# A decoder step on one Trainium2 core: the choice of the two experts and their weights moved from VectorE to GpSimd

## The chip, the core and the metric

The kernel runs on one core of a Trainium2 chip. The core has TensorE (PE in the profile; its weight loads are PEld), VectorE (DVE), ScalarE (ACT), GpSimd (POOL), SyncE (SP, here only a queue of DMAs) and 16 DMA engines, which share SBUF and PSUM. Each engine works through its own list of instructions in order and waits on semaphores for the others. The metric is the time of one execution on the device in microseconds; lower is better.

## What is computed

One layer of a decoder for 2048 prompt tokens and 8 decode tokens: a normalised and modulated input goes through one projection into a dilated sliding-window attention and a convolution, both halves are joined and projected out, and a mixture of 32 experts (4 groups of 8; the best group, in it the best 2) follows. The part that matters here, shortened:

```python
x = x + gt1 * (jnp.concatenate([att, conv], axis=-1) @ w_out)
h2 = rmsnorm(x, g_n2) * (1 + sc2) + sh2
lg = hf @ w_rg + b_rg                      # 4 group logits
pg = jax.nn.softmax(lg, axis=-1)
grp = jnp.argmax(lg, axis=-1)
le = (hf @ w_re + b_re).reshape(T, N_GROUPS, EXPERTS_PER_GROUP)[grp]
top_p, top_i = lax.top_k(jax.nn.softmax(le, axis=-1), TOP_K)
wts = p_grp * top_p / jnp.sum(top_p, axis=-1, keepdims=True)
eid = grp[:, None] * EXPERTS_PER_GROUP + top_i
```

Each token's two expert numbers (`eid`), their weights (`wts`) and its rank among the tokens of the same expert are kept; the rank gives the slot that the token's number is written to, from which the experts' stage gathers its rows.

## The kernel before

All matrices are float32, each split into a high and a low part that TensorE multiplies in three products. The kernel runs in stages; the change is in the fourth, `output_projection_and_routing`, between about 903 and 1222 us of the span.

This stage goes over 17 tiles: 16 of 128 prompt tokens and one of the 8 decode tokens. It is a software pipeline: `rounds` calls a body `round_(i)` for i from -1 to 19 on every engine, with i from 3 to 13 as a hardware loop. In round i each engine works on several tiles at once, in the order in which the calls are written:

- TensorE: the projection of tile i (`project`, L2217, 48 matmuls), the turn of the normed rows of tile i-1 (`turn_h2`, L2236), the ranks of tile i-2 (`ranks`, L2254 and L2255: a matmul over the sum `A` of the tile's two one-hot rows, and one over the counts so far), the turn of the convolution of tile i+2 (`turn_conv`, L2189), the turn of the mix of tile i+1 (`turn_mix`, L2206), the logits of tile i-1 (`logits`, L2246).
- VectorE: for tile i-1 the gating of the projection (`gated`, L1990, reads PSUM), for tile i-3 the weights (`weigh`), for tile i-1 the residual add (`added`, L1995), the low part of the turned attention (`att_rest`, L1967), for tile i-2 the logits and the routing (`take_logits`, L2013; `route`, L2027 to L2039), the swish (L1931, YT), for tile i-3 the rank and slot (`rank`), for tile i-2 the choice (`choose`), then the low part of the convolution (`conv_rest`, L1979), the moments of tile i+1 (`moments`, L1960 and L1963, into MV), norm and shift of tile i-1 (L1931 into H2, L1999), and the attention of tile i+1 (`branches`, `branch_shares`, `attended`, the last at L1956 into MIX).
- GpSimd: the kept weights of tile i-3, the scale of tile i-1 (`scale`, L1784, L1786), the normaliser of tile i+1 (`normalise`, L1772 to L1780, waits for the moments), the placing of tile i-3 (`place`: three copies and two indirect DMAs, L1814), the kept expert of tile i-2 (L1799), and inside the loop a DMA of zero rows (L1833). From round 15 on there is no normaliser.
- ScalarE: takes the turned tiles out of PSUM and splits off their high parts, the tanh and swish inputs, the squares (L1877), and for the routing two exponentials (`route_exps`), which give `EV` and `ZG`.

`choose` and `weigh` on VectorE are seven small instructions. `choose` makes the two expert numbers `EID` from the group `GF` and the indices `I8`, their one-hot rows `OH` and the sum `A`, and raises `picked`, for which TensorE's `ranks` and GpSimd's copy wait. `weigh` makes W1 = 1 / ((1 + EV) ZG) and W1 EV, and raises `w_done`. After the last tile the counts become the table of blocks (`experts_table`), with which the stage ends.

Of the kernel before, what the change touches and what calls it, by code (L numbers as in the profile page):

```python
# [17 lines left out]
P = 128  # L18
# [16 lines left out]
PER = 8  # L35
NEXP = GROUPS * PER
# [1556 lines left out]
def output_projection_and_routing(nc, t, dr, const, const_at, state):  # L1593
# [14 lines left out]
    def there(tile, last=TILES):  # L1608
        return not isinstance(tile, int) or 0 <= tile <= last

    def wait(engine, signal, value):
        if not (isinstance(value, int) and value <= 0):
            engine.wait_ge(signal, value)
# [7 lines left out]
    with ExitStack() as ctx:  # L1621
        def sb(name, shape, dt=F32):
            return ctx.enter_context(nc.sbuf_tensor(name, shape, dt))
# [4 lines left out]
        sem = stage_semaphores(nc, ctx)  # L1628
# [7 lines left out]
        BM, BE, BW, BT, BD, BRC = (sb("BM", [P, HEADS]), sb("BE", [P, 3, HEADS]), sb("BW", [P, 3, HEADS]), sb("BT", [P, 3, HEADS]), sb("BD", [P, HEADS]), sb("BRC", [P, HEADS]))  # L1636
        BS, MV, VE, RS, YT, TH = sb("BS3", [P, 6]), sb("MV3", [P, 2]), sb("VE3", [P, 1]), sb("RS3", [P, 1]), sb("YT3", [P, KC, P]), sb("TH3", [P, KC, P])
        MIX, MTH, MTL = sb("MIX", [P, D]), sb("MT_H", [P, KD, P], F32R), sb("MT_L", [P, KD, P], F32R)
        HA = KD // 2
# [10 lines left out]
        weight_kept, rank_kept, expert_kept, slot_copied = sem("weight_kept"), sem("rank_kept"), sem("expert_kept"), sem("slot_copied")  # L1650
        placing = sem("placing")
        NOROWS = sb("NOROWS", [P, D])
        BR = sb("BR", [P, NR])
# [24 lines left out]
        x2_out, h2_out, slot_out, count_psum, count_ready = sem("x2_out"), sem("h2_out"), sem("slot_out"), sem("count_psum"), sem("count_ready")  # L1678
        DECT = TILES

        with nc.Block() as block:
# [80 lines left out]
            def _(pool):  # L1762
                pool.iota(state["token"][:], [[P, ALLT]], base=0, channel_multiplier=1).then_inc(preset, 1)
                pool.memset(CNT[:], 0.0).then_inc(preset, 1)
                pool.memset(G8[:], -3e38).then_inc(preset, 1)
                pool.memset(NOROWS[:], 0.0).then_inc(norows_set, 1)
                for n in range(2):
                    pool.memset(SUMS[n][:], 0.0).then_inc(preset, 1)
# [19 lines left out]
                def column(name, i):  # L1788
                    return state[name][:, i:i + 1] if isinstance(i, int) else state[name][:, ds(i, 1)]

                def keep_weight(i):
                    pool.wait_ge(w_done, i + 1)
                    pool.sem_inc(placing, 1)
                    pool.tensor_copy(column("weight", i), W1[:, None, :]).then_inc(weight_kept, 1)

                def keep_expert(i):
                    pool.wait_ge(picked, i + 1)
                    pool.sem_inc(placing, 1)
                    pool.tensor_copy(column("expert", i), EID[:, None, :]).then_inc(expert_kept, 1)  # L1799

# [16 lines left out]
                def round_(i):  # L1817
                    if there(i - 3):
                        keep_weight(i - 3)
                    if there(i - 1):  # L1820
                        scale(i - 1)
                    if there(i + 1, TILES - 1):
                        normalise(i + 1)
                    if there(i - 3):
                        place(i - 3, rows_of(i - 3))
                    if there(i - 2):
                        keep_expert(i - 2)
                    if not isinstance(i, int):

                        pool.wait_ge(norows_set, 1)  # L1830
                        first = pool.snap(i * (3 * P) + (NEXP - 3 * 3) * P)
                        pool.sem_inc(placing, 1)
                        pool.dma_start(dr["y"][ds(first, 3 * P)].rearrange("(b p) d -> p b d", p=P),  # L1833
                                       NOROWS[:, None, :].to_broadcast([P, 3, D])).then_inc(norows_out, 16)

# [5 lines left out]
            def _(act):  # L1841
# [10 lines left out]
                def take_conv(i):  # L1852
                    if isinstance(i, int) and i == DECT:

# [28 lines left out]
                def route_exps(i):  # L1883
                    act.wait_ge(gmax_ready, i + 1)
                    nc.scalar.activation(GE[:], LOG[:, 0:GROUPS], ACT.Exp, bias=NG[:], scale=1.0, accum_out=ZG[:]).then_inc(group_exp, 1)
                    act.wait_ge(gap_ready, i + 1)
                    nc.scalar.activation(EV[:], DV[:], ACT.Exp).then_inc(gap_exp, 1)
# [41 lines left out]
            def _(dve):  # L1929
# [84 lines left out]

                RST = 9

                def route(i):
# [3 lines left out]
                    def step(ins):  # L2021
                        at[0] += 1
                        ins.then_inc(rstep, 1)
                        dve.wait_ge(rstep, i * RST + at[0])

                    dve.wait_ge(logits_taken, i + 1)
                    step(nc.vector.tensor_copy(G8[:, 0:GROUPS], LOG[:, 0:GROUPS]))  # L2027
                    nc.vector.memset(PAUSE[:], 0.0)
# [11 lines left out]
                    assert at[0] == RST  # L2040

                def choose(i):
                    nc.vector.tensor_copy(I2[:], I8[:, 0:2]).then_inc(cstep, 1)
                    dve.wait_ge(cstep, i * 5 + 1)
                    wait(dve, expert_kept, i)
                    stt(EID[:], GF[:].to_broadcast([P, 2]), float(PER), I2[:], ALU.mult, ALU.add).then_inc(cstep, 1)
                    dve.wait_ge(cstep, i * 5 + 2)
                    nc.vector.tensor_tensor(OH[:], const("iota")[:, None, :].to_broadcast([P, 2, NEXP]), EID[:, :, None].to_broadcast([P, 2, NEXP]), ALU.is_equal).then_inc(cstep, 1)
                    dve.wait_ge(cstep, i * 5 + 3)
                    nc.vector.tensor_tensor(A[:], OH[:, 0], OH[:, 1], ALU.add).then_inc(picked, 1)  # L2050

                def weigh(i):
                    dve.wait_ge(gap_exp, i + 1)
                    wait(dve, weight_kept, i)
                    stt(DEN[:], EV[:], 1.0, ZG[:], ALU.add, ALU.mult).then_inc(cstep, 1)
                    dve.wait_ge(cstep, i * 5 + 4)
                    nc.vector.reciprocal(W1[:, 0:1], DEN[:]).then_inc(cstep, 1)
                    dve.wait_ge(cstep, i * 5 + 5)
                    nc.vector.tensor_tensor(W1[:, 1:2], W1[:, 0:1], EV[:], ALU.mult).then_inc(w_done, 1)

# [67 lines left out]
                def round_(i):  # L2128
                    if there(i - 1):
                        gated(i - 1, rows_of(i - 1), which_of(i - 1))  # L2130
                    if there(i - 3):
                        weigh(i - 3)
                    if there(i - 1):
# [8 lines left out]
                    if there(i - 3):  # L2142
                        rank(i - 3, rows_of(i - 3))
                    if there(i - 2):
                        choose(i - 2)
                    if isinstance(i, int) and i == 0:
# [785 lines left out]
```

## Time and profile before

| | before |
|---|---|
| median of 3 runs | 2150.32 us |
| lowest, highest | 2149.15, 2156.6 us |
| the profiled execution, its own time | 2152.61 us |
| span of its instructions | 2151.1 us |
| busy: PE, PEld | 1979.5 us (92%), 1587.9 us (74%) |
| busy: DVE, ACT, POOL | 1564.6 us (73%), 1051.0 us (49%), 530.8 us (25%) |

The span runs from the first to the last instruction of the profiled execution. Shares over the whole span mix stages with different limits, so the stage of the change is read by itself: in windows (busy time of each engine in a stretch) and in timelines (an engine's instructions in order of time, equal ones merged, with the idle time ahead of them and what ended it in brackets).

### The profile page before, as it was taken

Reading aid. Unit: us, or ns where it says so; the run is one execution under the profiler, and the core shown is the slowest. Engines: PE = TensorE matmul, PEld = TensorE weight load, DVE = VectorE, ACT = ScalarE, POOL = GpSimd, SP = SyncE. Lnnn points to the kernel's source line nnn. Section 1 sums busy time; section 2 is a strip of 40 time slices with the busy share of each in tenths; the row PEclk is TensorE's granted clock in tenths of the full one; section 3 lists DMA queues with packets and bytes.
Section 4 is the critical chain, followed back from the end, with each engine's and each line's share of the span. In section 5 each row is a group of like instructions: output and inputs, shape, how many; then the busy total and the mean of one; then the engine's idle time right before and its main releaser. Section 6 shows DMA issues by size and latency. Waiting matters only on the chain. (4 is left out here: it accounts for less than half of the span.)

```text
span 2151.1 us, 40123 instructions
## 1 busy us (share of the span) xinstructions
PE 1979.5 (92%) x13273; PEld 1587.9 (74%) x13274; DVE 1564.6 (73%) x3061; ACT 1051.0 (49%) x2056; POOL 530.8 (25%) x569
## 2 busy tenths in 40 slices
PE   5999999998999999689999499999999999999986
PEld 3788888886787777378888478788787877878732
DVE  2648898887788888289998678664637576558747
ACT  2411111111888888045444277555536575557533
POOL 1013454331111144015564300101010101000155
PEclk8999999999999999789999699999999999999978
DMA  8786555674759488767877299974848798769967
GB/s 255 240 289 247 186 195 188 210 254 146 234 149 309 151 286 293 239 220 231 275 251 270 78 347 398 343 292 179 295 163 327 267 360 306 273 223 395 391 222 310
DMA packets 221489, 553.19 MB, mean 257 GB/s; under 512 B 28978, under 2 KB 43658, under 8 KB 220105
## 3 DMA queue, kind: packets, MB, share of 16 engines
q1 hardware_dynamic: 171131, 425.60, 56.5%
q0 software_dynamic: 25024, 75.71, 9.7%
q10 hardware_dynamic: 25239, 50.67, 6.8%
q8 instruction: 52, 0.85, 0.2%
q14 instruction: 43, 0.35, 0.1%
HBM read 456.95 MB, written 167.56 MB: 290 GB/s over the span
## 5 line engine op out<-in xcount | busy, mean ns | idle before, releaser
L2546 DVE TENSOR_TENSOR LO<-WIDE,HI 128x2048 fp32r<-128x2048 f32 x128 | 287.1, 2284 | 82.2 <-ACT HI L2468 82.2
L647 DVE SCALAR_TENSOR_TENSOR arena<-arena,tapw 128x512 f32<-128x512 f32 (+3 forms) x435 | 266.3, 690 | 0.0
L2468 ACT CAST HI<-WIDE 128x2048 fp32r<-128x2048 f32 x128 | 238.5, 1910 | 24.0 <-PEq L220 15.7
L448 POOL TENSOR_TENSOR STATS<-STATS,K 128x1 f32<-128x1 f32 x16 | 135.2, 8451 | 308.4 <-ACT H L500 308.4
L2546 DVE TENSOR_TENSOR LO<-W2E,HI 128x2048 fp32r<-128x2048 f32 x64 | 143.8, 2288 | 92.1 <-ACT HI L2468 92.1
L780 PE MATMUL PJ<-WIN_H,HTH 128*128 128x512 f32 x640 | 160.5, 393 | 5.0 <-ACT HTH L508 5.0
L790 PE MATMUL PJ<-WIN_L,HTH 128*128 128x512 f32 x640 | 158.7, 390 | 0.0
L784 PE MATMUL PJ<-WIN_H,HTL 128*128 128x512 f32 x640 | 158.2, 389 | 0.0
L2468 ACT CAST HI<-W2E 128x2048 fp32r<-128x2048 f32 x64 | 118.8, 1904 | 60.1 <-issue 60.1
L780 PEld LDWEIGHTS PJ<-WIN_H,HTH 128*128 128x128 f32 x640 | 118.8, 188 | 33.1 <-issue 9.2
L532 ACT ACTIVATE arena<-PJ 128x512 f32<-128x512 f32 x48 | 28.6, 601 | 231.6 <-PE PJ L790 231.6
L784 PEld LDWEIGHTS PJ<-WIN_H,HTL 128*128 128x128 f32 x640 | 120.2, 188 | 25.2
L790 PEld LDWEIGHTS PJ<-WIN_L,HTH 128*128 128x128 f32 x640 | 119.8, 188 | 25.5 <-issue 0.8
L2421 POOL DMA_INDIRECT XG<-h_rows,IDX x40 | 44.8, 1121 | 366.2 <-PE XP L2605 338.3
L1281 PE MATMUL TB<-K,PR 128*128 128x128 f32 x600 | 81.1, 278 | 8.6 <-ACT PTS L1163 8.2
L2621 PE MATMUL YP<-HI,GH 128*128 128x512 f32 x320 | 84.1, 405 | 4.6
L1176 ACT ACTIVATE PR<-MOD_,ML 128x256 f32<-128x256 f32 (+1 forms) x192 | 86.5, 461 | 1.3 <-PE TB L1281 0.8
L2834 PE MATMUL SUM<-Y,SHARE 128*128 128x512 f32 (+1 forms) x136 | 69.7, 665 | 18.4 <-DMA Y<-expert_rows,dest 16.1
L2616 PE MATMUL AE<-HI,XH 128*128 128x512 f32 x320 | 80.3, 393 | 6.8 <-issue 6.8
L2506 ACT CAST GH<-GP 128x256 fp32r<-128x256 f32 x80 | 29.8, 372 | 114.8 <-PE GP L2611 112.3
L1176 ACT ACTIVATE PR<-SBX,ML 128x256 f32<-128x256 f32 (+1 forms) x192 | 85.8, 453 | 0.0
L2417 POOL DMA_DIRECT2D IDX<-slot_tokens x40 | 23.1, 576 | 247.4 <-issue 247.4
(375 smaller groups left out, 4489.4 us busy)
## 6 DMA issues: line engine op xcount, KB each, us to landing
WIDE<-in_w_expert_gate SPq DMA_DIRECT2D x64, 1024.0 KB, 8.4
WIDE<-in_w_expert_up SPq DMA_DIRECT2D x64, 1024.0 KB, 9.9
W2E<-in_w_expert_down SPq DMA_DIRECT2D x64, 1024.0 KB
expert_rows<-YE ACTq DMA_DIRECT2D x40, 512.0 KB, 6.2
expert_rows<-NOROWS POOLq DMA_DIRECT2D x11, 1536.0 KB
QN<-q_rows SPq DMA_DIRECT2D x48, 256.0 KB
KN<-out_new_k_prompt SPq DMA_DIRECT2D x48, 256.0 KB, 4.9
VN<-out_new_v_prompt SPq DMA_DIRECT2D x48, 256.0 KB, 4.7
```

Source lines behind the costliest of these rows:

```text
L448: pool.tensor_tensor(MS[:], SSQ[:], const("eps"), ALU.add).then_inc(ms_ready, 1)
L647: ins = nc.vector.scalar_tensor_tensor(out=out, in0=src, scalar=tap, in1=out, op0=ALU.mult, op1=ALU.add)
L780: nc.tensor.matmul(PJ[:, n], HTH[:, k], WH[:, n, k], start=k == 0, stop=False)
L784: nc.tensor.matmul(PJ[:, n], HTL[:, k], WH[:, n, k], start=False, stop=False)
L790: mm = nc.tensor.matmul(PJ[:, n], HTH[:, k], WL[:, n, k], start=False, stop=k == KD - 1)
L1176: ins = nc.scalar.activation(PR[hh][:, h, 0:w], SBX[hh][:, h, 0:w], ACT.Exp, bias=ML[g.q][:, head:head + 1], scale=-1.0, accum_out=ML[g.q] ...
L1281: mm = nc.tensor.transpose(TB[u % 2][:, n], PR[head // HH][:, head % HH, k * P:(k + 1) * P], const("ident"))
L2468: nc.scalar.copy(HI[n][:, cols], raw[n][:, cols]).then_inc(hi_ready[n], 1)
L2546: nc.vector.tensor_tensor(LO[n][:, cols], raw[n][:, cols], HI[n][:, cols], ALU.subtract).then_inc(lo_ready[n], 1)
L2616: mm = nc.tensor.matmul(out, x[:, k], w[n][:, k * DEXP:(k + 1) * DEXP], start=first and k == 0, stop=last and k == KD - 1)
L2621: mm = nc.tensor.matmul(YP[:, half * 512:half * 512 + 512], g[:, k], w[2][:, k * D + half * 512:k * D + half * 512 + 512], start=first and ...
L2834: mm = nc.tensor.matmul(SUM[0:r, n % SUMS, cols], SHARE[0:r, n % SUMS, which, 0:r], y[0:r, n % DEEP, cols], start=which == 0, stop=which == 1)
```

## The change

`choose` and `weigh` leave VectorE's program. GpSimd does both for tile i-2, at the end of its round, behind the placing of tile i-3, and keeps expert and weight right behind each. The weights are now made one round earlier in program order than before. GpSimd's forms are simpler, so there are more: `choose` is the cast of the indices, the group times 8, their sum (EID), two one-hot comparisons of 32 columns, their sum (A), and the copy of the expert; `weigh` is an add, a product, a power of -1, a product, and the copy. VectorE's `route` gets a wait for `picked` of the tile before, ScalarE's `route_exps` one for `w_done` of the tile before. A tile of 128 bytes per partition (MIXPLACE), which nothing reads or writes, lies ahead of MIX, MT_H and MT_L, so these and all behind them lie 128 bytes further; four small tiles and two semaphores are added.

```diff
@@ -1635,6 +1635,7 @@
+        PLACED = sb("MIXPLACE", [P, 32])
         MIX, MTH, MTL = sb("MIX", [P, D]), sb("MT_H", [P, KD, P], F32R), sb("MT_L", [P, KD, P], F32R)
...
@@ -1788,14 +1795,43 @@
-                def keep_weight(i):
+                def weigh(i):
+
+                    pool.wait_ge(gap_exp, i + 1)
+                    pool.sem_inc(placing, 1)
+                    pool.tensor_tensor(ONEPLUS[:], EV[:], const("ones")[:, 0:1], ALU.add).then_inc(weigh_step, 1)
+                    pool.wait_ge(weigh_step, i * 3 + 1)
+                    pool.tensor_tensor(DEN[:], ONEPLUS[:], ZG[:], ALU.mult).then_inc(weigh_step, 1)
+                    pool.wait_ge(weigh_step, i * 3 + 2)
+                    wait(pool, weight_kept, i)
+                    pool.sem_inc(placing, 1)
+                    pool.tensor_tensor(W1[:, 0:1], DEN[:], MINUS[:], ALU.pow).then_inc(weigh_step, 1)
+                    pool.wait_ge(weigh_step, i * 3 + 3)
+                    pool.tensor_tensor(W1[:, 1:2], W1[:, 0:1], EV[:], ALU.mult).then_inc(w_done, 1)
                     pool.wait_ge(w_done, i + 1)
                     pool.sem_inc(placing, 1)
                     pool.tensor_copy(column("weight", i), W1[:, None, :]).then_inc(weight_kept, 1)
 
-                def keep_expert(i):
-                    pool.wait_ge(picked, i + 1)
+                def choose(i):
+
+                    pool.wait_ge(rstep, i * RST + RST)
                     pool.sem_inc(placing, 1)
+                    pool.tensor_copy(I2[:], I8[:, 0:2]).then_inc(cstep, 1)
+                    pool.tensor_tensor(GROUP8[:], GF[:], EIGHT[:], ALU.mult).then_inc(cstep, 1)
+                    pool.wait_ge(cstep, i * 5 + 2)
+                    wait(pool, expert_kept, i)
+                    wait(pool, slot_ready, i)
+                    pool.sem_inc(placing, 1)
+                    pool.tensor_tensor(EID[:], I2[:], GROUP8[:].to_broadcast([P, 2]), ALU.add).then_inc(cstep, 1)
+                    pool.wait_ge(cstep, i * 5 + 3)
+                    wait(pool, kstep, i * 2)
+                    pool.sem_inc(placing, 1)
+                    for n in range(2):
+                        pool.tensor_scalar(OH[:, n], const("iota"), EID[:, n:n + 1], None, ALU.is_equal).then_inc(cstep, 1)
+                    pool.wait_ge(cstep, i * 5 + 5)
+                    wait(pool, counted, i)
+                    pool.sem_inc(placing, 1)
+                    pool.tensor_tensor(A[:], OH[:, 0], OH[:, 1], ALU.add).then_inc(picked, 1)
                     pool.tensor_copy(column("expert", i), EID[:, None, :]).then_inc(expert_kept, 1)
...
@@ -1815,8 +1851,6 @@
                 def round_(i):
-                    if there(i - 3):
-                        keep_weight(i - 3)
                     if there(i - 1):
                         scale(i - 1)
...
                     if there(i - 2):
-                        keep_expert(i - 2)
+                        choose(i - 2)
+                        weigh(i - 2)
...
@@ -1882,6 +1917,7 @@
                     act.wait_ge(gmax_ready, i + 1)
+                    wait(act, w_done, i)
...
@@ -2024,6 +2058,7 @@
                     dve.wait_ge(logits_taken, i + 1)
+                    wait(dve, picked, i)
...
```

VectorE's own `choose` and `weigh` (L2042 to L2059 of the kernel before) and their two calls in its round go.

VectorE, the first round behind the loop (rounds inside it read alike but for register rows), from the swish to the moments, before:

```order
L1931 SCALAR_TENSOR_TENSOR YT<-TH,YT 128x512
L2064 TENSOR_TENSOR CNT<-CNT,AR 128x32
L2065 TENSOR_TENSOR RSEL<-OH,SMALL 128x64
L2068 TENSOR_REDUCE R<-RSEL 128x2
L1931 SCALAR_TENSOR_TENSOR SLOT<-EID,R 128x2
L2043 CAST I<-I 128x2
L1931 SCALAR_TENSOR_TENSOR EID<-GF,I 128x2
L2048 TENSOR_TENSOR OH<-K,EID 128x64
L2050 TENSOR_TENSOR AR<-OH 128x32
L1979 TENSOR_TENSOR MT_L<-YT,MT_H 128x512
L1960 BN_STATS BS<-CP 128x6
```

and after:

```order
L1967 SCALAR_TENSOR_TENSOR YT<-TH,YT 128x512
L2080 TENSOR_TENSOR CNT<-CNT,AR 128x32
L2081 TENSOR_TENSOR RSEL<-OH,SMALL 128x64
L2084 TENSOR_REDUCE R<-RSEL 128x2
L1967 SCALAR_TENSOR_TENSOR SLOT<-EID,R 128x2
L2015 TENSOR_TENSOR MT_L<-YT,MT_H 128x512
L1996 BN_STATS BS<-CP 128x6
```

The four instructions of the choice are gone; the three of the weights, between L1990 and L1995, are gone likewise.

GpSimd, inside the loop, from the placing to the DMA of zero rows, before (ISA and REGISTER_ALU rows are its sequencer's waits and sums):

```order
L1808 COPY SLOTP<-SLOT 128x2
L1809 REGISTER_ALU
L1809 COPY rank<-R 128x2
L1814 DMA slot_tokens<-TOK,SLOTP 69632x1 x2
L1797 REGISTER_ALU
L1799 ISA
L1799 COPY expert<-EID 128x2
L1833 ISA
L1833 DMA expert_rows<-NOROWS 128x3x1024
```

and after, from the same two DMAs to the sum that TensorE waits for, and the first of the weights:

```order
L1850 DMA slot_tokens<-TOK,SLOTP 69632x1 x2
L1817 ISA
L1819 CAST I<-I 128x2
L1820 TENSOR_TENSOR GROUP<-GF,PERGROUP 128x1
L1821 ISA
L1825 TENSOR_TENSOR EID<-I,GROUP 128x2
L1826 REGISTER_ALU
L1613 REGISTER_ALU
L1830 TENSOR_SCALAR OH<-K,EID 128x32 x2
L1831 REGISTER_ALU
L1834 TENSOR_TENSOR AR<-OH 128x32
```

The choice now comes behind the two DMAs of the placing. TensorE's order is what it was: its rank matmul over AR stands between the turn of the normed rows and the turns of the convolution and of the mix.

## Rows read from the trace of the kernel before

**Rows 1.** Windows: busy us (instructions) of each engine; granted clock, DMA share, GB/s.

```profile
1000.00:1100.00 100.00, 98.35 (x559) 83.83 (x558) 94.40 (x290) 47.75 (x117) 57.73 (x88) 1.00 0.78 257
```

**Rows 2.** Timeline, TensorE, a steady round: start us, us, instruction, [idle <-releaser].

```profile
1062.46 0.31 PE L2254 MATMUL SMALL<-AR,K 128*128 128x32 f32 x2
...
1063.75 1.06 PE L2206 MATMUL TPS<-K,MIX 128*128 128x128 f32 x8 [0.29 <-issue]
```

**Rows 3.** Timeline, TensorE, the first round with a rank, and tile 12's rank.

```profile
967.05 0.31 PE L2254 MATMUL SMALL<-AR,K 128*128 128x32 f32 x2
...
968.76 1.87 PE L2246 MATMUL SMALL<-WR,H2T 128*128 128x36 f32 x16
...
981.69 1.04 PE L2236 MATMUL HPS<-K,H 128*128 128x128 f32 x8
982.56 0.31 PE L2254 MATMUL SMALL<-AR,K 128*128 128x32 f32 x2
...
1158.49 0.31 PE L2254 MATMUL SMALL<-AR,K 128*128 128x32 f32 x2
```

**Rows 4.** Timeline, VectorE, a steady round.

```profile
1048.75 0.15 DVE L1931 SCALAR_TENSOR_TENSOR DEN<-EV,ZG 128x1 f32<-128x1 f32 x1
...
1049.21 1.23 DVE L1995 TENSOR_TENSOR X<-X 128x1024 f32<-128x1024 f32 x1
...
1050.95 0.18 DVE L2013 TENSOR_TENSOR LOG<-SMALL,BR 128x36 f32<-128x36 f32 x1
...
1054.69 0.16 DVE L2043 CAST I<-I 128x2 f32<-128x2 uint32 x1
...
1055.46 0.69 DVE L1979 TENSOR_TENSOR MT_L<-YT,MT_H 128x512 fp32r<-128x512 f32 x1
...
1056.80 0.18 DVE L1963 BATCH_NORM_AGGREGATE MV<-BS 128x2 f32<-128x6 f32 x1
...
1062.96 0.69 DVE L1956 TENSOR_TENSOR MIX<-NB 128x512 f32<-128x512 f32 x1
1063.60 1.23 DVE L1990 TENSOR_TENSOR X<-OP,GATE 128x1024 f32<-128x1024 f32 x1
```

**Rows 5.** Timeline, GpSimd, the same round.

```profile
1057.06 1.18 POOL L1772 TENSOR_TENSOR VE<-MV,K 128x1 f32<-128x1 f32 x1 [2.28 <-DVE MV L1963]
...
1063.44 1.05 POOL L1814 DMA_INDIRECT slot_tokens<-TOK,SLOTP  x1 [0.31 <-issue]
1064.49 0.20 POOL L1799 COPY expert<-EID 128x2 f32 x1
...
1065.56 0.92 POOL L1794 COPY weight<-W1R 128x2 f32 x1
1069.43 0.71 POOL L1784 TENSOR_TENSOR MS<-SSQ,K 128x1 f32<-128x1 f32 x1 [2.96 <-ACT SQ L1877]
```

**Rows 6.** GpSimd: timeline with VectorE idle; groups by form (busy us, mean ns | idle).

```profile
912.09 0.19 POOL L1772 TENSOR_TENSOR VE<-MV,K 128x1 f32<-128x1 f32 x1 [6.88 <-DVE MV L1963]
912.35 0.55 POOL L1775 TENSOR_TENSOR RS<-VE,K 128x1 f32<-128x1 f32 x1
...
L1038 POOL TENSOR_TENSOR DPR<-dec_k,WAD 128x768 f32<-128x768 f32 x8 | 14.6, 1819 | 12.2 <-DVE SC L1085 12.2
```

**Rows 7.** Timeline, TensorE, behind an idle time in the experts' stage.

```profile
2044.15 0.69 PE L2611 MATMUL GP<-K,GE 128*128 128x128 f32 x2 [2.71 <-DVE GE L2565]
...
2045.40 3.02 PE L2621 MATMUL YP<-HI,GH 128*128 128x512 f32 x8
2048.25 2.00 PE L2621 MATMUL YP<-HI,GL 128*128 128x512 f32 x8
```

**Rows 8.** Timelines, TensorE and GpSimd, last tile.

```profile
1210.26 0.63 PE L2254 MATMUL SMALL<-AR,K 8*128 8x32 f32 x2 [4.08 <-DVE AR L2050]
...
1212.81 0.19 POOL L1799 COPY expert<-EID 128x2 f32<-128x2 f32 x1
```

More of the change, by code:

```diff
@@ L1651, in output_projection_and_routing @@
         placing = sem("placing")
+        EIGHT, MINUS, ONEPLUS, GROUP8 = sb("PERGROUP", [P, 1]), sb("MINUSONE", [P, 1]), sb("ONEPLUS", [P, 1]), sb("GROUP8", [P, 1])
+        amounts_set, weigh_step = sem("amounts_set"), sem("weigh_step")
         NOROWS = sb("NOROWS", [P, D])
@@ L1679, in output_projection_and_routing @@
         DECT = TILES
+        RST = 9
         with nc.Block() as block:
@@ L1766, in _ @@
                 pool.memset(NOROWS[:], 0.0).then_inc(norows_set, 1)
+                pool.memset(EIGHT[:], float(PER)).then_inc(amounts_set, 1)
+                pool.memset(MINUS[:], -1.0).then_inc(amounts_set, 1)
+                pool.wait_ge(amounts_set, 2)
                 for n in range(2):
@@ L2013, in take_logits @@
                     nc.vector.tensor_tensor(LOG[:], LP[:], BR[:], ALU.add).then_inc(logits_taken, 1)
-                RST = 9
                 def route(i):
@@ L2040, in route @@
                     assert at[0] == RST
[L2042 to L2059, printed above, removed]
                 def rank(i, rows):
@@ L2130, in round_ @@
                         gated(i - 1, rows_of(i - 1), which_of(i - 1))
-                    if there(i - 3):
-                        weigh(i - 3)
                     if there(i - 1):
@@ L2143, in round_ @@
                         rank(i - 3, rows_of(i - 3))
-                    if there(i - 2):
-                        choose(i - 2)
                     if isinstance(i, int) and i == 0:
```

## The prediction

> **What bounds the kernel now.** I read the windows by engine first, then the timelines of the stage "output projection and routing" (903 to 1222 us of the span) engine by engine. The windows show that TensorE and VectorE are both nearly full there, at the full clock, while GpSimd has 42% of its time free [rows 1]. That invites moving small VectorE work to GpSimd. The timelines say who holds the round. The stage runs one round per tile of 128 tokens. I count rounds by the start of the rank matmul: tile 0's at 967.05, tile 12's at 1158.49, twelve rounds in 191.4 us, 15.95 us each [rows 3]. TensorE pauses once in a round, before it turns the mix: that starts at 1063.75, 0.1 us after VectorE has ended the mix (1062.96 + 0.69) [rows 2, 4]. In the first of the twelve rounds this pause is absent, and TensorE needs 15.51 us to the next rank matmul (967.05 to 982.56 [rows 3]). VectorE's rows show no gap in a steady round. So VectorE is the bound by a small margin: 15.95 against TensorE's 15.51. Shortening VectorE can save at most 0.44 us a round, some 5 us over the twelve.
>
> **What leaves VectorE.** The three instructions of the weights take 0.46 us (1048.75 to 1049.21) and the four of the choice 0.77 us (1054.69 to 1055.46) [rows 4]. That is 1.23 us a round, nearly three times the 0.44 it can be paid for.
>
> **What comes onto GpSimd, and where.** The choice of tile i-2 now stands behind the placing of tile i-3, whose two indirect DMAs end at 1064.49 [rows 5]. But TensorE wants the rank matmul of that very tile at 1062.46 [rows 2], 2.0 us before GpSimd even begins, and this matmul reads the sum of the one-hot rows that the choice produces. Before, VectorE had it ready at 1055.46. Behind the waiting rank matmul TensorE's queue holds the turn of the convolution, the turn of the next mix, the logits and the next projection. So a new wait stands in the main chain, and it feeds itself: logits release VectorE's routing, that reaches the moments, those release GpSimd's normalise, then the placing, then the next choice. I add up this loop from one rank matmul, at r, to the next:
> - TensorE, rank to end of logits: 967.05 to 968.76 + 1.87, 3.6 us [rows 3].
> - VectorE, logits taken to moments ready: 1050.95 to 1056.80 + 0.18 is 6.03 us, less the 0.77 of the choice: 5.26, so r + 8.9 [rows 4].
> - GpSimd, moments ready to the end of the second indirect DMA: 1056.98 to 1064.49, 7.5 us, r + 16.4 [rows 5]. Nothing in it changes, since VectorE does beside it what it did before.
> - The choice. The trace has no such GpSimd instructions, so I bound it. A free GpSimd instruction on one or two columns takes 0.19 us [rows 6]; 768 columns take 1.82 us, so 32 columns add 0.07. Seven instructions in five dependent steps, 0.08 us between steps, come to about 1.3 us. That is the lower end. But GpSimd's small instructions are held while VectorE runs a large operation on two operands in SBUF: the same kind of first step takes 1.18 us beside one and 0.19 free, and the copy of the weights takes 0.92 us beside the residual add (which began at 1065.2, as it did at 1049.21 one round before) [rows 4 to 6]. The copy of the expert, beside the gating that reads PSUM, is not held: 0.19 [rows 5]. The gating starts at 1063.60 [rows 4] and, with the weights gone, the residual add follows 1.25 us later, at 1064.85 to 1066.08. The first two instructions fit in front of it, the third (the expert's number) would start at about 1064.9 and is held to 1066.1; the one-hot rows and their sum then take 0.8 with VectorE idle. End at 1066.9: 2.4 us. I take this, as the copy of the weights is the nearest row. As upper end I take 3.0.
> - TensorE starts within 0.1.
>
> The sum is 3.6 + 5.26 + 7.5 + 2.4 + 0.1 = 18.9 us a round instead of 15.95. Twelve rounds: 227 less 191.4, **+35 us**. The weights on GpSimd (five instructions, one of them a power at 0.55 us, some 1.8 in all) lie behind the choice; GpSimd then waits for ScalarE's squares, as it does today for 2.96 us [rows 5], with 2.9 us more in the longer round, so they cost nothing. ScalarE's new wait for the weights is 5 us behind them. VectorE's new wait before routing is for a choice that TensorE has already waited for.
>
> The last rounds have no normalise, so GpSimd comes to the choice early: tiles 13 and 14 find no wait, and the round to tile 13 drops its pause, -0.8 us. The last tile waits again: its rank matmul started at 1210.26, right after VectorE's choice, while GpSimd ends placing at 1212.81 [rows 8] and needs 1.3 us for the choice: 1214.1, +3.8 us, and the block table is behind it. Together without the clock: 35.4 - 0.8 + 3.8 = **+38 us**.
>
> The Trainium skill (GPSIMD Engine Reference, section 4.1, Engine selection) puts two-input elementwise work on GpSimd at about twice VectorE's time. By that the choice would take 2 x 0.77 = 1.5 us, a round 18.0, and the sum without the clock would be some +28 us; the held copy in this trace speaks for more than a factor of two, and the row decides.
>
> **The clock.** TensorE ends turning the normed rows at r + 14.64 + 1.04 = r + 15.7 [rows 3], so it would idle 3.2 us in every round. After an idle time of 2.71 us the next matmuls ran at the lower level: eight 512-column ones took 3.02 us against 2.00 us for the next eight, and the six transposes ahead of them 1.25 against about 0.8; some 1.5 us lost, then full speed again [rows 7]. I take the 0.8 from the eight transposes of the normed rows, 1.04 us at the full clock [rows 3]. What follows the idle time here (rank, turns, logits) is the part of TensorE's work that is on the loop, the projection behind it has slack. I take 1.5 us in four of five rounds, about 14 us (all twelve: 18; none: 0).
>
> **The mix tile's move** by 128 bytes changes no instruction and no count; TensorE's eight transposes and the two writers of that tile show no row that depends on where it lies. I take 0; on TensorE's projection even a few ns per matmul would now be hidden by the idle time.
>
> **Forecast.** 38 + 14 = +52 us. The profiled execution took 2152.61 us (span 2151.1), 2.3 above the median of 2150.32 of three runs; against the median, **2202 us**.
>
> **Rivals.**
> 1. The clock stays up, since the idle time is short of what lets it fall each time. For it: a round has 15 us of dense matmuls. Against it: the row of 2.71 us [rows 7]. 2150.3 + 38 = 2188 us.
> 2. GpSimd is not held in the choice (its instructions slip in between VectorE's): 1.3 us, a round of 17.8, TensorE idle 2.1 us. Twelve rounds +22, with the ends +25: 2175 us. The tight start of the third instruction speaks for it, the copy at 0.92 against it.
> 3. Not slower: the choice is ready before TensorE asks. It decides at 1062.46; GpSimd would have to end placing by 1061.1 instead of 1064.49. If the placing shrank by 3.4 us with a freer VectorE, TensorE alone would set the round: 12 x 0.45 = 5 us less, 2145 us. Against it: the two DMAs overlap the same VectorE work as before, as the loop gives VectorE nothing to skip there.
> 4. Each step on GpSimd is dearer than its rows (one-hot with a per-partition scalar, which no row shows): choice 3.0 us and the clock down in each round: 19.5 + 1.5, some +64: 2214 us; at 0.3 us more in each of its steps, 2222.
>
> **Chances.** Forecast 0.54, rival 1 0.22, rival 2 0.08, rival 3 0.05, rival 4 0.11. A measurement of this kernel tells a change from none at about 0.5%, 11 us. Only rival 3 is within that or faster: slower 0.95, same 0.04, faster 0.01. The range from 2174 to 2222 takes in rivals 1, 2 and 4 and leaves out rival 3 and the tails.
>
> **What would show it.** Right: TensorE's rank matmul waits about 3 us for GpSimd's AR in every round from tile 1 to 12; the rounds are 18 to 21 us long; the expert's number on GpSimd takes over 1 us; VectorE has gaps before the high-low split of the mix; the granted clock of the stage falls below 1.0; outside the stage nothing moves. Wrong: rounds of 15.5 us with no idle time ahead of the rank matmul would mean that the placing ends sooner than I say; no slow logits after the idle time would give the clock's 14 us back; a choice of over 3 us would mean that I priced GpSimd's instructions too low.

## The result, and the profile after

| | before | after |
|---|---|---|
| median | 2151.64 us (4 runs) | 2231.38 us (4 runs) |
| lowest, highest | 2149.15, 2156.6 us | 2229.16, 2237.38 us |
| the profiled execution, its own time | 2152.61 us | 2237.38 us |
| span of its instructions | 2151.1 us | 2235.8 us |

The ratio is 1.037, 95% interval 1.034 to 1.040: slower by 80 us, where I had forecast 52 (2202 us) and at most 72 (2222 us). The direction and the place were right, the size was not. The profiled execution of after is the slowest of its four, 6 us above their median, so its rows add up to 85 us more than before, not 80.

The page of after: span; busy time, share and instructions of each engine.

```profile
span 2235.8 us, 40327 instructions
...
PE 2017.2 (90%) x13273; PEld 1624.9 (73%) x13274; DVE 1552.9 (69%) x2942; ACT 1051.5 (47%) x2056; POOL 570.9 (26%) x741
```

GpSimd has 40 us more to do and VectorE 12 less. TensorE is 38 us "busier" with the same work, which means that part of it ran at the lower clock. Windows of the stage, before and then after, and 100 us in its middle, after (columns as in [rows 1]):

```profile
903.00:1222.00 319.00, 276.25 (x1495) 233.74 (x1495) 271.81 (x811) 130.68 (x304) 140.67 (x234) 0.92 0.69 228
```

```profile
905.00:1310.00 405.00, 317.07 (x1495) 273.12 (x1495) 259.30 (x691) 130.63 (x304) 185.97 (x406) 0.81 0.54 180
1000.00:1100.00 100.00, 86.14 (x400) 74.55 (x400) 67.01 (x184) 31.95 (x80) 51.97 (x106) 0.85 0.51 176
```

In the middle, where TensorE and VectorE were nearly full [rows 1], VectorE now has a third of its time free and TensorE 14%; the granted clock has gone from 1.00 to 0.85. The waits of after from 950 to 1230 us say for what (us in total, times, longest):

```profile
PE SMALL L2266 <- POOL AR L1834: 39.1, 12, 4.6
...
DVE LOG L2049 <- PE SMALL L2258: 16.7, 13, 2.0
```

TensorE's rank matmul waits twelve times for GpSimd's sum of the one-hot rows in this stretch: 0.42 us for tile 0, then 0.90 to 4.61 for tiles 1 to 11 (tile 12's, 2.75, lies behind it). Over tiles 1 to 12 that is 3.45 us on average, and 0.90 and 2.16 in two of the rounds. One round in the timeline of TensorE, after:

```profile
1037.17 0.63 PE L2266 MATMUL SMALL<-AR,K 128*128 128x32 f32 x2 [4.54 <-POOL AR L1834]
...
1038.92 1.92 PE L2218 MATMUL TPS<-K,MIX 128*128 128x128 f32 x8
1040.63 3.47 PE L2258 MATMUL SMALL<-WR,H2T 128*128 128x36 f32 x16
1043.90 3.27 PE L2229 MATMUL OP<-WO_H,MT_H 128*128 128x512 f32 x8
1047.01 2.01 PE L2229 MATMUL OP<-WO_H,MT_L 128*128 128x512 f32 x8
...
1056.11 1.03 PE L2248 MATMUL HPS<-K,H 128*128 128x128 f32 x8
1060.25 0.63 PE L2266 MATMUL SMALL<-AR,K 128*128 128x32 f32 x2 [3.10 <-POOL AR L1834]
```

Behind the idle time the transposes (1.92, in [rows 2] 1.06), the logits (3.47, in [rows 3] 1.87) and most of the first eight projection matmuls (3.27) run at about half speed. VectorE in the same round, up to the moments, and its gating and residual add:

```profile
1044.22 0.20 DVE L2049 TENSOR_TENSOR LOG<-SMALL,BR 128x36 f32<-128x36 f32 x1 [1.97 <-PE SMALL L2258]
...
1049.46 0.18 DVE L1999 BATCH_NORM_AGGREGATE MV<-BS 128x2 f32<-128x6 f32 x1
...
1056.49 1.23 DVE L2026 TENSOR_TENSOR X<-OP,GATE 128x1024 f32<-128x1024 f32 x1 [0.17 <-PE OP L2229]
1057.75 1.22 DVE L2031 TENSOR_TENSOR X<-X 128x1024 f32<-128x1024 f32 x1
```

GpSimd in the same round, from the second indirect DMA to the sum:

```profile
1056.14 1.01 POOL L1850 DMA_INDIRECT slot_tokens<-TOK,SLOTP  x1 [0.30 <-issue]
1057.17 0.19 POOL L1819 CAST I<-I 128x2 f32<-128x2 uint32 x1
1057.32 0.18 POOL L1820 TENSOR_TENSOR GROUP<-GF,PERGROUP 128x1 f32<-128x1 f32 x1
1057.70 0.19 POOL L1825 TENSOR_TENSOR EID<-I,GROUP 128x2 f32<-128x2 f32 x1 [0.20 <-POOL GROUP L1820]
1058.19 1.37 POOL L1830 TENSOR_SCALAR OH<-K,EID 128x32 f32<-128x32 f32 x2 [0.30 <-POOL EID L1825]
1059.77 0.25 POOL L1834 TENSOR_TENSOR AR<-OH 128x32 f32<-128x32 f32 x1 [0.21 <-POOL OH L1830]
```

The loop reads straight off these rows: rank at 1037.17, logits taken 1044.22 (7.05), moments ready 1049.64 (5.42), second DMA done 1057.15 (7.51), sum ready 1060.02 (2.87), next rank 1060.25 (0.23): 23.1 us. The twelve rounds from tile 0 (971.84) to tile 12 (1237.07) take 265.2 us, 22.1 each and 20.1 to 23.5 one by one, where I had 20.1 on average.

### The profile page after: what moved, and what is told of

It is laid out like the page before. It is cut to its first block and busy times, and to the rows that moved or that the text cites. A ratio compares the mean times of both kernels' runs of the same rounds, so it can differ in the third digit from the quotient of the medians.

```text
span 2235.8 us, 40327 instructions
## 1 busy us (share of the span) xinstructions
PE 2017.2 (90%) x13273; PEld 1624.9 (73%) x13274; DVE 1552.9 (69%) x2942; ACT 1051.5 (47%) x2056; POOL 570.9 (26%) x741
## 5 line engine op out<-in xcount | busy, mean ns | idle before, releaser
L2229 PE MATMUL OP<-WO_H,MT_H 128*128 128x512 f32 x272 | 83.7, 458 | 0.8 <-ACT MT_H L1885 0.8
L2846 PE MATMUL SUM<-Y,SHARE 128*128 128x512 f32 (+1 forms) x136 | 65.4, 628 | 20.1 <-DMA Y<-expert_rows,dest 20.1
```

The lines of the kernel that those rows point to most:

```text
L2229: mm = nc.tensor.matmul(OP[:, n * 512:(n + 1) * 512], x[:, k], w[:, k, n * 512:(n + 1) * 512], start=start and k == ks[0], stop=stop and k ...
```

## The experiments

All are compared with the kernel before, run beside them on the same chip (medians 2151.8 to 2152.0 us). "r" is the start of the rank matmul.

**1. The clock taken out.** `warm` is the kernel after with 14 extra 512-column matmuls ahead of the rank matmul, on data that is already there; their results are not used.

```diff
+                def fill(i):
+                    pe.wait_ge(y_norm, i + 2)
+                    for k in range(FILL):
+                        nc.tensor.matmul(CP[:].rearrange("p c t -> p (c t)"), MTH[:, k % KD], WOH[:, k % KD, 0:512], start=True, stop=True)
...
+                    if there(i + 2, TILES - 1) and there(i - 2):
+                        fill(i)
                     if there(i - 2):
                         ranks(i - 2, rows_of(i - 2))
```

> The changed kernel with 14 matmuls of 512 columns (into a PSUM tile that is free at that place, results unused) put between TensorE's turn of the normed rows and its rank matmul, in the rounds that wait for GpSimd. They fill about 3.2 us of the idle time of 3.1 to 4.6 us. If the lower clock behind the idle time is what the forecast lacked: from rank matmul to logits taken falls from a mean of 5.98 us to about 3.8 in all rounds, twelve rounds shorten by some 26 us, time near 2203 us (ratio to before 1.02 to 1.03); the granted clock of the stage is near 1. If the clock is only a sign of the waiting and costs nothing by itself (rival), the time stays at 2231 us within 5.

Measured: 2214.4 us (2210.68 to 2215.88), ratio 1.028 [1.027, 1.030]. TensorE of warm, and the third step of its choice on GpSimd:

```profile
1045.77 3.45 PE L2266 MATMUL CP<-WO_H,MT_H 128*128 128x512 f32 x14
1050.57 0.40 PE L2273 MATMUL SMALL<-AR,K 128*128 128x32 f32 x2 [1.34 <-POOL AR L1835]
...
1052.38 1.87 PE L2259 MATMUL SMALL<-WR,H2T 128*128 128x36 f32 x16
```

```profile
1047.75 1.10 POOL L1826 TENSOR_TENSOR EID<-I,GROUP 128x2 f32<-128x2 f32 x1 [0.20 <-POOL GROUP L1821]
```

The clock stays up, the logits take 1.87 us, and the rounds are regular: 20.1 us, all but the first and the last within 0.03. So the clock costs 2.0 us of 22.1 a round. That is 24 us over the twelve rounds of the two profiled executions, about the 26 expected, and 17 us between the medians; the expected 2203 us was 11 too low. With the clock out, 20.1 can be held against my 18.9 term by term: r to logits taken 3.81 (I had 3.6), logits to moments 5.42 (5.26), moments to second DMA 7.53 (7.5), choice 3.13 (2.4), start 0.23 (0.1). Of the 1.2 us excess, 0.7 is the choice.

**2. One part alone: choice, or weights.** In `choose_only` GpSimd makes the choice as in after, and the three instructions of the weights are back on VectorE between gating and residual add. `weigh_only` is the other half: the choice back on VectorE in its old place, the weights at the end of GpSimd's round. Both keep the 128-byte tile.

```diff
                     if there(i - 2):
                         choose(i - 2)
-                        weigh(i - 2)
```

```diff
                     if there(i - 2):
-                        choose(i - 2)
+                        keep_expert(i - 2)
                         weigh(i - 2)
```

> The changed kernel with the weights back on VectorE as before, so that only the choice is made by GpSimd, behind the placing. By the theory of the place the loop has all that it had: 2231 us within 6, rounds of 20 to 23 us. If the weights on GpSimd had a part in the loss (they stand behind the choice and ahead of the next scale), it comes out more than 10 us below.

> The changed kernel with the choice back on VectorE as before, so that only the weights are made by GpSimd, at the end of its round; the mix stays 128 bytes further. By the theory of the place nothing on TensorE's chain waits for GpSimd here. VectorE loses 0.46 us a round (16.0 to about 15.55), TensorE with the shifted tiles needs 15.3, so VectorE still sets the round, at about 15.55: twelve rounds save 5 us, 2146 us, ratio 0.997 to 0.998. If GpSimd's five more instructions delay its normalise or its scale (rival: GpSimd as such is the trouble), rounds of 16 us or more and no gain: 2151 or above.

Measured: `choose_only` 2231.49 us (2228.65 to 2237.27), 1.037 [1.035, 1.039], the time of after; `weigh_only` 2148.15 us (2145.55 to 2151.26), 0.998 [0.997, 0.999]. Both came out as expected, weigh_only 2 us above the 2146. The whole loss is the choice's. TensorE of choose_only, and of weigh_only:

```profile
1032.89 0.40 PE L2265 MATMUL SMALL<-AR,K 128*128 128x32 f32 x2 [4.30 <-POOL AR L1822]
...
1035.55 3.47 PE L2257 MATMUL SMALL<-WR,H2T 128*128 128x36 f32 x16
```

```profile
1044.51 0.31 PE L2260 MATMUL SMALL<-AR,K 128*128 128x32 f32 x2
...
1045.72 1.06 PE L2212 MATMUL TPS<-K,MIX 128*128 128x128 f32 x8 [0.21 <-issue]
```

The twelve rounds of weigh_only are 15.66 us on average instead of 15.95 (in the steady part 15.69 instead of 16.00), since VectorE, the bound, has 0.46 us less. The round gains only 0.3 of these: the residual add now starts 1.26 us behind the gating, where the first instruction of the weights had started 1.14 behind it (1047.61 and 1048.75), and the logits are taken 0.05 us later behind the low part of the attention.

**3. The 128 bytes.** `pad_only` is the kernel before with the tile MIXPLACE, `no_pad` the kernel after without it, `weigh_no_pad` is weigh_only without it.

```diff
+        PLACED = sb("MIXPLACE", [P, 32])
```

> The kernel before with the mix, its turned parts and all behind them 128 bytes further, nothing else. If the place of the tiles matters for TensorE's reads (the changed kernel's eight projection matmuls take 1.98 us against 2.02): the same 1.98 here; TensorE gains 0.24 us a round but VectorE holds the round at 15.95, so the time is the same, within 2 us of 2151.6. If the shorter matmuls come from the longer round instead, they stay 2.02 here. If the shift cost something in itself: above 2155 us.

> The changed kernel without the 128 bytes ahead of the mix. TensorE's projection matmuls go back from 1.98 to 2.02 us for eight (1.5 us more for all 48 of two rounds), but TensorE idles 3 to 4.6 us a round, so the time stays within 5 us of 2231. It moves up only if the idle time matters less than I think.

> The weights alone on GpSimd, without the 128-byte tile. The gain of this move was so far seen together with the tile (rounds 15.69 us, ratio 0.998). Theory A, the gain is VectorE's: it is gapless and has 0.46 us less to do in either kernel, so the rounds are again about 15.7 us, 2148 us, ratio 0.998. Theory B, the tile is needed: eight projection matmuls take 2.02 instead of 1.98 us, TensorE alone then needs 15.5 us to the next rank matmul, and a pause at the turn of the mix of 0.1 to 0.3 us comes on top; rounds of 15.8 us or more, 2149.5 us, ratio 0.999. Either way the eight matmuls read 2.02 us.

Measured: pad_only 2151.39 us, 1.000 [0.999, 1.001]; no_pad 2236.59 us (2230.52 to 2239.31), 1.038 [1.036, 1.040], not told apart from after (5.2 us above the expected 2231, with 5 allowed); weigh_no_pad 2149.24 us, 0.9985 [0.998, 0.999], and rounds of 15.70. TensorE of pad_only, then of weigh_no_pad:

```profile
1053.90 1.98 PE L2218 MATMUL OP<-WO_H,MT_L 128*128 128x512 f32 x8
...
1065.38 1.06 PE L2207 MATMUL TPS<-K,MIX 128*128 128x128 f32 x8 [0.53 <-issue]
```

```profile
1051.69 2.02 PE L2222 MATMUL OP<-WO_H,MT_L 128*128 128x512 f32 x8
...
1062.83 1.07 PE L2211 MATMUL TPS<-K,MIX 128*128 128x128 f32 x8
```

The tile does something that I had not seen: eight projection matmuls take 1.98 instead of 2.02 us, 0.2 us a round. In pad_only that is given straight back: the pause at the mix grows from 0.29 [rows 2] to 0.53, as VectorE holds the round. In weigh_no_pad the pause is gone, in weigh_only it is 0.21; VectorE has no gap in either, and the rounds are the same, 15.70 and 15.69. So the gain of the weights' move is VectorE's (Theory A), and without the tile TensorE has nothing left to spare.

**4. The order on GpSimd.** `choice_before_place` puts the choice between normalise and placing, `choice_first` ahead of normalise too.

```diff
+                    if there(i - 2):
+                        choose(i - 2)
                     if there(i - 3):
                         place(i - 3, rows_of(i - 3))
                     if there(i - 2):
-                        choose(i - 2)
                         weigh(i - 2)
```

> The changed kernel with the choice moved on GpSimd from behind the placing to between normalise and placing (the weights stay at the end). Theory of the place in the queue: the loop from rank to rank loses the placing's 4.5 us, 3.6 + 5.4 + 3 + 3 = 15 us, less than TensorE's own 15.5, so the wait and with it the low clock vanish: 2145 to 2155 us. Rival (GpSimd's small instructions cost because they are on GpSimd, held by VectorE's large operations, wherever they stand): still more than 2190 us.

> The same with the choice ahead of normalise, right behind the scale, where GpSimd idled 2.3 us before. By the theory of the place TensorE never waits for the choice, VectorE is shorter by 1.23 us a round, and TensorE alone sets the round at 15.5 us: 5 us less than before, 2146 us, ratio 0.996 to 0.999. What could spoil it: normalise comes up to 1.3 us later and ScalarE's mix is late for TensorE's turn (it has over 2 us). By the rival (cost of GpSimd itself): above 2190 us.

Measured: choice_before_place 2163.47 us (2161.54 to 2164.23), 1.005 [1.003, 1.007]; choice_first 2154.13 us (2151.3 to 2158.16), 1.001 [1.000, 1.002]. Both expectations were too low, by 8 us or more. With the choice between normalise and placing, the rounds are 16.83 us; GpSimd, and TensorE behind it:

```profile
1014.35 1.75 POOL L1825 TENSOR_TENSOR EID<-I,GROUP 128x2 f32<-128x2 f32 x1 [0.20 <-POOL GROUP L1820]
1016.39 1.33 POOL L1830 TENSOR_SCALAR OH<-K,EID 128x32 f32<-128x32 f32 x2 [0.30 <-POOL EID L1825]
```

```profile
1018.41 0.40 PE L2267 MATMUL SMALL<-AR,K 128*128 128x32 f32 x2 [1.25 <-POOL AR L1834]
```

The wait shrinks from 3.45 us on average to 1.25 but does not go, since here both steps of the choice are held by VectorE: from cast to sum it takes 4.37 us (1013.82 to 1018.19), where the expectation had 3. In choice_first no rank matmul waits; TensorE waits elsewhere instead, for 1.0 to 1.2 us in about every other round and 0.3 to 0.6 in the others:

```profile
1032.24 0.63 PE L2202 MATMUL CP<-K,CC 128*128 128x128 f32 x4 [1.18 <-ACT MIX L1937]
```

The normaliser now stands behind the choice on GpSimd; ScalarE's MIX, which applies it and reads the PSUM tile CP, comes late, and so does the turn of the convolution, which writes CP anew. It is the old trap again: a step moved off the path of one wait is put ahead of another.

**5. The order on TensorE.** `rank_late` is after with the rank matmuls behind the logits; `late_and_before` has both orders changed.

```diff
-                    if there(i - 2):
-                        ranks(i - 2, rows_of(i - 2))
                     if isinstance(i, int) and i == -1:
                         turn_mix(0)
...
                     if there(i - 1):
                         logits(i - 1)
+                    if there(i - 2):
+                        ranks(i - 2, rows_of(i - 2))
```

> The changed kernel with one edit on TensorE: the rank matmuls stand behind the logits instead of ahead of the two turns. GpSimd's program is untouched, the choice is as late as in the changed kernel, but only the next projection is queued behind the wait. The loop from rank to rank then is about 0.6 (rank to logits taken) + 5.4 + 7.5 + 3.1 + 0.1 = 16.7 us, the idle time ahead of the rank 1.4 us, too short for the lower clock: about 12 x 0.75 us over before and a few at the end, 2160 to 2166 us. If GpSimd's lateness itself cost, and not what is queued behind the wait, the time stays above 2200 us.

> After with both orders changed: on GpSimd the choice ahead of the placing, the weights behind it; on TensorE the rank matmuls behind the logits. If the loss is only the one loop from rank matmul over logits, moments and choice back to the rank matmul, it now has 3 us less than with the rank late alone (17.1 us a round) and 5 us more time than with the choice earlier alone (16.8): no wait of the rank matmul is left, TensorE never stops for over 0.5 us, the clock stays at 1.00, and the rounds are 15.6 to 15.8 us: 2146 to 2149 us. The rival: GpSimd itself is then full (its small instructions held beside VectorE's large ones), its normalise and placing come later, and VectorE or the turn of the mix waits for that: rounds of 16.2 us or more, 2154 us.

Measured: rank_late 2171.86 us (2169.78 to 2174.28), 1.009 [1.008, 1.011], rounds of 17.1 us; late_and_before 2156.97 us (2155.39 to 2163.04), 1.003 [1.002, 1.004], steady rounds of 16.06. Both expectations were too low. The late rank was to come to 2160 to 2166 us, as its idle time would be too short for the lower clock, and it was not too short. The rounds of late_and_before lie between its two forecasts (15.6 to 15.8, and the rival's 16.2 or more), and the waits of VectorE below are the rival's. In rank_late three quarters of the loss are gone, because the logits no longer stand behind the wait:

```profile
1019.35 1.97 PE L2258 MATMUL SMALL<-WR,H2T 128*128 128x36 f32 x16
1022.54 0.40 PE L2266 MATMUL SMALL<-AR,K 128*128 128x32 f32 x2 [1.22 <-POOL AR L1834]
...
1023.12 3.67 PE L2229 MATMUL OP<-WO_H,MT_H 128*128 128x512 f32 x8
```

What is left is the wait of 1.22 us, in every second round, and behind it the first eight projection matmuls at 3.67 us instead of 2.10. In late_and_before no rank matmul waits inside the loop and the clock is 1.00, yet the round is 0.37 us longer than in weigh_only. VectorE and GpSimd there:

```profile
1056.41 1.28 DVE L1968 SCALAR_TENSOR_TENSOR H<-X,RSTD,GAIN 128x1024 f32<-128x1024 f32 x1 [0.53 <-POOL RSTD L1793]
...
1059.93 1.76 DVE L1989 TENSOR_TENSOR NB<-NB,BT 128x1536 f32<-128x1536 f32 x1
```

```profile
1059.99 1.75 POOL L1825 TENSOR_TENSOR EID<-I,GROUP 128x2 f32<-128x2 f32 x1 [0.20 <-POOL GROUP L1820]
```

GpSimd has become part of the bound: its scale comes 0.53 us late for VectorE, which also waits 0.32 us for the logits. So even with the shortest rounds of the four orders tried, the choice on GpSimd costs more than the 0.77 us that it takes off VectorE; choice_first has longer rounds (16.18 on average against 16.04) and the shorter time, 2154.13 us, and that too is 6 us above weigh_only.

## Why the prediction was right, and where it was wrong

The new wait and its loop were forecast as they came. What failed is the size of two of the sum's terms, above all the price of the clock, set at 14 us: the runs show 25 in the twelve rounds and 4 more in the round behind them. The choice, set at 2.4 us a round, takes 3.0. Rival 4, and with it the upper end of my range, 2222 us, allowed for the dearer choice, but for no more than 1.5 us a round of the clock. The times measured, over the twelve rounds of the profiled executions and beside them:

| | forecast, us | measured, us |
|---|---|---|
| first rank matmul (967.05 to 971.84) | 0 | +4.8 |
| twelve rounds, over 191.4 | +35 and +14 | +73.8 |
| round to tile 13 | -0.8 | +3.8 |
| rounds to tiles 14 and 15 | 0 | +1.7 |
| last tile | +3.8 | +4.5 |
| behind the stage's last rank matmul | 0 | -3.8 |
| sum, of the unrounded terms | +52 | +84.7 |

- **The bound, and what it can give back: right.** weigh_only takes 0.46 us from VectorE and gains 0.29 a round, within the 0.44 that I gave as the most.
- **The new loop and its place: right.** The rank matmul waits for AR in all twelve rounds, 3.45 us on average (I had about 3), VectorE idles ahead of the high-low split, and with another order of the choice against the placing, or of the rank against the logits, three quarters of the loss or more are gone (experiments 4 and 5). Of the signs that I named, three did not come true as written: the rounds go up to 23.5 us and not 21, the expert's number takes over 1 us in six of the twelve only, and the core reached the stage 1.7 us later. Rival 3 fell: GpSimd ends placing 7.5 us behind the moments, as I had it.
- **The choice: the mechanism right, the size wrong, 0.6 us a round, some 7 us in all.** I had 2.4; it takes 2.2 free, and 2.9 to 3.2 in nearly every round, 3.0 on average. I put 0.8 us for the two one-hot rows and their sum, behind the held expert's number (by my own rates it should have been 0.94: 0.08 + 0.52 + 0.08 + 0.26). Free, they take 1.41: 0.23 + 0.72 + 0.21 + 0.25. That is the whole 0.6. The rows of tile 13's choice and weights, with VectorE idle:

```profile
1252.58 0.19 POOL L1825 TENSOR_TENSOR EID<-I,GROUP 128x2 f32<-128x2 f32 x1 [0.20 <-POOL GROUP L1820]
1253.01 0.72 POOL L1830 TENSOR_SCALAR OH<-K,EID 128x32 f32<-128x32 f32 x2 [0.23 <-POOL EID L1825]
1253.93 0.25 POOL L1834 TENSOR_TENSOR AR<-OH 128x32 f32<-128x32 f32 x1 [0.21 <-POOL OH L1830]
...
1254.27 0.18 POOL L1802 TENSOR_TENSOR ONEPLUS<-EV,K 128x1 f32<-128x1 f32 x1
1254.53 0.19 POOL L1804 TENSOR_TENSOR DEN<-ONEPLUS,ZG 128x1 f32<-128x1 f32 x1
1254.93 0.57 POOL L1808 TENSOR_TENSOR W1R<-DEN,MINUSONE 128x1 f32<-128x1 f32 x1 [0.20 <-POOL DEN L1804]
```

 The gaps show what my 0.08 had missed. It came from steps with nothing but waits between them, and there it holds: 0.08 between ONEPLUS and DEN. Between DEN and W1R, and between all three pairs of steps of the choice, the program also has a `sem_inc(placing, 1)`, and the gap is 0.17 to 0.30. This split holds in every round of after; no run leaves the increment out, so that it is the cause is not shown.

 The holding by the residual add I had right. Which instruction it hits depends on a few tenths: EID where it starts just behind the add's start (VectorE, then GpSimd, one round earlier), else the one-hot rows, as at 1058.19 above.

```profile
1034.19 1.22 DVE L2031 TENSOR_TENSOR X<-X 128x1024 f32<-128x1024 f32 x1
```

```profile
1034.37 1.10 POOL L1825 TENSOR_TENSOR EID<-I,GROUP 128x2 f32<-128x2 f32 x1 [0.20 <-POOL GROUP L1820]
```

 EID ends at 1035.47, 0.06 behind the add's 1035.41. The Trainium skill (GPSIMD Engine Reference, section 1, Specifications) says that GpSimd's way to SBUF contends with VectorE instructions that have two SBUF inputs; these rows agree. The Trainium skill's factor of about two for two-input work (the same page, section 4.1, Engine selection) is too small for such short steps: 2.2 us free against 0.77 is 2.8 times, 3.13 held is 4.1 times.
- **The clock: wrong by about 0.9 us a round, 11 us over the twelve.** I took 1.2 us a round from a place where 512-column matmuls follow the idle time [rows 7]. Here rank, turns and logits follow, and the low level lasted through them: r to logits taken is 3.81 with the clock up and 7.05 where it was down throughout, 5.92 on average, so 2.1 us a round against 1.2. Nine of the twelve rounds have it, near my four of five; it is the price that was wrong, 2.8 us in each of them and not 1.5. Rival 4's "clock down in each round" charged no more than that either, though at half speed all 3.6 us of rank to logits could double. Experiment 1 confirms the size: 2.0 us.
- **The three small terms of the base: 0.5 us a round.** r to logits taken is 3.81, since I summed to the end of the logits and left out VectorE's start (0.2); VectorE's way to the moments shrank by 0.61 us and not by the choice's 0.77, since the choice's first instruction had overlapped the slot (1054.61 and 1054.69), while the low part of the convolution starts only 0.23 behind it; TensorE starts 0.2 behind the sum, not 0.1.
- **The round to tile 13: wrong, +3.8 instead of -0.8.** Its rank matmul does not wait, as I said. But tile 12's did (2.75 us), and what follows was slow, projection included:

```profile
1237.07 0.41 PE L2266 MATMUL SMALL<-AR,K 128*128 128x32 f32 x2 [2.75 <-POOL AR L1834]
...
1239.24 3.47 PE L2258 MATMUL SMALL<-WR,H2T 128*128 128x36 f32 x16
1242.52 3.76 PE L2229 MATMUL OP<-WO_H,MT_H 128*128 128x512 f32 x8
1246.08 2.81 PE L2229 MATMUL OP<-WO_H,MT_L 128*128 128x512 f32 x8
```

 I had stopped the clock's price at the twelfth round, though the wait ahead of it is the twelfth's.
- **The last tile: right** (+4.5 for +3.8; in after its rank matmul waits 9.00 us for GpSimd, the round is 13.5 us for 9.0), though the free choice in it takes 2.15 us and not 1.3. Tile 15's rank matmul, of which I said nothing, waits 2.44 us; its round is 2.0 us longer. The start of the stage (+4.8) I had not looked at: 1.7 us of it came before the stage began, and 2.5 are the first projection behind 941.72, whose first two groups of eight matmuls took 3.75 and 3.03 us, against 2.10 and 2.02 before. It is slow in the profiles of choose_only and no_pad too, and in no other run's; nothing tried here says why.
- **Weights on GpSimd at no cost: right.** choose_only and after have one time. **The mix tile at 0: right for the time, wrong in the reason.** I saw no row that could depend on it, and the projection's does, by 0.04 us in eight; VectorE hides it.

The misses in the twelve rounds (clock 11, choice 7, base 6) make up, within rounding, the 24 us by which 265.2 exceeds 241.

## What to carry to other kernels

Before moving a small step to an engine with free time, ask which wait of the full engines reads its result, and lay out that loop by starts and ends: GpSimd's free 42% was no help, since its queue came to the choice only after TensorE had asked for it, and a step that saved VectorE 0.77 us made the round 6 us longer. If TensorE idles in the loop, price everything on the loop behind the idle time at the lower clock, for as long as it is small matmuls, and take that as the range's end. Of two steps to be moved, try each alone: the one that nobody waits for (the weights) was worth its move (0.998), the other was not in any order tried.

## What the runs showed of the hardware

- Between dependent small instructions on GpSimd lie 0.07 to 0.09 us where only waits stand between them (ONEPLUS and DEN; also the steps of the normaliser and the scale), and 0.16 to 0.30 where the program also has a `sem_inc` there and nothing else holds them up; instructions with no wait between them follow at once (1057.17 and 1057.32).
- A GpSimd instruction of 0.19 us that starts while a large VectorE instruction with two operands in SBUF runs ends within 0.06 us of that one's end: 1.75 us beside the product of 1536 columns (1059.99 + 1.75 = 1061.74, the product's end is 1061.69).
- Idle times of 1.25 us (choice_before_place, behind the projection and the turn of the normed rows) and 1.34 (warm, behind 14 large matmuls) left TensorE's clock up; 1.22 us behind the turns and the logits (rank_late) was followed by eight matmuls in 3.67 us instead of 2.10. In these rows the length of the idle time alone does not tell whether the clock falls.
- 128 bytes in the place of the projection's tiles change eight 512-column matmuls from 2.02 to 1.98 us, in each pair with and without the tile. The cause was not looked for.
